# Three whole weight slots in a two-layer diffusion backbone: the low part overwrites the raw weights

## What is computed

```python
for i in range(2):
    m_l = silu(c) @ w_mod[i] + b_mod[i]            # shift, scale, gate, twice
    a_l = rmsnorm(x, norm_mix_g[i]) * (1 + sc1) + sh1
    # i == 0: z = a @ w_in -> q, k, v, g; chunked GLA both ways; o = rmsnorm(o) * silu(g); y = o @ w_out
    # i == 1: z = a @ w_in -> y, u; conv; r, i gates = sigmoid(u @ gate weights); linear scan; y = (h * gelu(y)) @ w_out
    x = x + g1 * y_l
    f_l = rmsnorm(x, norm_ffn_g[i]) * (1 + sc2) + sh2
    x = x + g2 * ((silu(f_l @ w1) * (f_l @ w3)) @ w2)
    # the context stream: the same in layer 0; in layer 1 it only feeds the scan
```

## Time and profile before

| | |
|---|---|
| median of three runs | 1799.82 us |
| the profiled execution | 1797.24 us |
| its span | 1795.3 us |
| PE busy | 1668.3 us (93%) |
| POOL busy | 603.3 us, of which 582.9 in `low` |
| ACT busy | 516.1 us, of which 192.4 in `high` |
| DVE busy | 609.2 us |
| granted PE clock, mean | 0.964 of full |
| DMA | 89 GB/s over the span |

### The profile page before, as it was taken

One profiled execution on the slowest core, in us unless ns is written; L12 is line 12 of the kernel. 1 busy time (PEld: TensorE's weight loads), 2 busy tenths in 40 slices (PEclk: granted clock), 3 DMA queues, 4 the chain that ended last, 5 costly groups with the idle time before them and its releaser, 6 DMA issues. The chain is left out here.

```text
span 1795.3 us, 22539 instructions
## 1 busy us (share of the span) xinstructions
PE 1668.3 (93%) x9980; PEld 1400.0 (78%) x9980; DVE 609.2 (34%) x700; ACT 516.1 (29%) x559; POOL 603.3 (34%) x434
## 2 busy tenths in 40 slices
PE   4799999998979999999999998899986799999997
PEld 2587888886868888888888887688865688888886
DVE  3733343434351121012110214758786412012122
ACT  3524141413132110111111113377772321122122
POOL 1221212212313233323322335244373355444453
PEclk9899999999989999999999999899997899999999
DMA  7242323223214332233322332022122132333322
GB/s 286 72 118 71 95 71 95 71 71 90 87 35 127 109 118 85 66 109 111 113 83 71 113 96 74 24 71 70 49 69 71 47 94 96 95 107 102 94 76 76
DMA packets 197492, 160.63 MB, mean 89 GB/s; under 512 B 7202, under 2 KB 193940, under 8 KB 197396
## 3 DMA queue, kind: packets, MB, share of 16 engines
q1 hardware_dynamic: 197396, 159.20, 28.7%
HBM read 157.08 MB, written 2.10 MB: 89 GB/s over the span
## 5 line engine op out<-in xcount | busy, mean ns | idle before, releaser
L490 POOL TENSOR_TENSOR w_lo<-raw,w_hi 128x512 fp32r<-128x512 f32 (+1 forms) x404 | 582.9, 1473 | 1165.1 <-ACT w_hi L918 1165.1
L534 PE MATMUL duo<-a_hi,w_hi 128*128 128x512 f32 (+1 forms) x1664 | 503.2, 363 | 52.9 <-DVE a_lo L1300 19.1
L540 PE MATMUL duo<-a_hi,w_lo 128*128 128x512 f32 (+1 forms) x1664 | 494.1, 357 | 0.0
L537 PE MATMUL duo<-a_lo,w_hi 128*128 128x512 f32 (+1 forms) x1664 | 493.0, 357 | 0.0
L534 PEld LDWEIGHTS duo<-a_hi,w_hi 128*128 128x128 f32 x1664 | 275.8, 192 | 116.4 <-issue 51.4
L918 ACT ACTIVATE w_hi<-raw 128x2048 fp32r<-128x2048 f32 (+1 forms) x101 | 192.4, 1905 | 590.4 <-PE duo L540 590.3
L537 PEld LDWEIGHTS duo<-a_lo,w_hi 128*128 128x128 f32 x1664 | 275.8, 192 | 47.7
L540 PEld LDWEIGHTS duo<-a_hi,w_lo 128*128 128x128 f32 x1664 | 274.4, 192 | 46.2
L1491 DVE TENSOR_TENSOR hid<-duo,gate 128x1024 f32<-128x1024 f32 (+1 forms) x33 | 33.5, 1043 | 540.3 <-PE duo L540 540.3
L534 PE MATMUL duo<-h_hi,w_hi 128*128 128x512 f32 (+1 forms) x528 | 160.8, 358 | 0.1
L540 PE MATMUL duo<-h_hi,w_lo 128*128 128x512 f32 (+1 forms) x528 | 158.8, 355 | 0.0
(11 more groups left out here) (211 smaller groups left out, 1502.5 us busy)
## 6 DMA issues: line engine op xcount, KB each, us to landing
raw<-in_ffn_w_dram SPq DMA_DIRECT2D x120, 512.0 KB, 4.9
mod_ring<-in_w_mod_dram SPq DMA_DIRECT2D x80, 512.0 KB, 5.2
raw<-in_gla_w_in_dram SPq DMA_DIRECT2D x24, 512.0 KB, 4.6
mod_first<-in_w_mod_dram SPq DMA_DIRECT2D x8, 1024.0 KB, 15.0
raw<-in_lru_w_in_dram SPq DMA_DIRECT2D x16, 512.0 KB, 4.2
raw<-in_ffn_w_dram SPq DMA_DIRECT2D x16, 384.0 KB, 3.8
raw<-in_gla_w_out_dram SPq DMA_DIRECT2D x8, 512.0 KB, 4.8
raw<-in_lru_w_out_dram SPq DMA_DIRECT2D x8, 512.0 KB, 4.5
```

The source lines that it names most:

```text
L490: pool.tensor_tensor(w_lo[b][:, k:k + 2, 0:cols], raw[b][:, k:k + 2, 0:cols], w_hi[b][:, k:k + 2, 0:cols].bitcast(F32), ALU.subtract).then ...
L534: pe.matmul(tile_out(ps, t, part, n), wh, act_hi[:, k, s:s + n], start=opens, stop=False, skip_group_check=True)
L537: pe.matmul(tile_out(ps, t, part, n), wh, act_lo[:, k, s:s + n], start=False, stop=False, skip_group_check=True)
L540: mm = pe.matmul(tile_out(ps, t, part, n), wl, act_hi[:, k, s:s + n], start=False, stop=last, skip_group_check=True)
```

## The change

Three slots instead of two. A slot is now a `raw` buffer, which the low part overwrites in place, and a `w_hi` buffer: 3 x 16 KB, the same 48 KB. `load` of chunk ch now waits until PE is done with chunk ch - 3. `high` waits for the load alone. The wait of `high` for `y_done` in an LRU block moves down to the GELU that reads the result. `low` handles a 768-row chunk in three instructions, not four, and rounding covers no more than the chunk has. The order of all the programs stays.

```diff
-        counts.append((counts[ch - 2] if ch >= 2 else 0) + (64 if name[0] == "lg" else 32))
+        counts.append((counts[ch - 3] if ch >= 3 else 0) + (64 if name[0] == "lg" else 32))
...
-        raw = [place(f"raw{b}", [P, 8, 256], F32, W_AT + 8 * KB * b) for b in range(2)]
-        w_hi = [place(f"w_hi{b}", [P, 8, 256], F32R, W_AT + 8 * KB * (2 + b)) for b in range(2)]
-        w_lo = [place(f"w_lo{b}", [P, 8, 256], F32R, W_AT + 8 * KB * (4 + b)) for b in range(2)]
+        raw = [place(f"raw{b}", [P, 8, 256], F32, W_AT + 8 * KB * b) for b in range(3)]
+        w_hi = [place(f"w_hi{b}", [P, 8, 256], F32R, W_AT + 8 * KB * (3 + b)) for b in range(3)]
+        w_lo = [place(f"w_lo{b}", [P, 8, 256], F32R, W_AT + 8 * KB * b) for b in range(3)]
...
+        HEIGHT = [6 if name[0] == "w2" and name[2] == 2 else 8 for name in CH]
+        LOWS = list(itertools.accumulate([0] + [h // 2 for h in HEIGHT]))
+        USERS = [("tlow" if name == "gate1" else name + (3,) if name[0] == "lg" else name) for name in CH]
...
-                if ch >= 2:
-                    sp.wait_ge(lo_ready, 4 * (ch - 1))
+                if ch >= 3:
+                    used = USERS[ch - 3]
+                    if used[0] == "ly" and used[1] < BLOCKS - 1:
+                        sp.wait_ge(y_done, used[1] + 1)
+                    else:
+                        wait_done(sp, used)
                 for dst, src in pieces:
-                    sp.dma_start(dst, src).then_inc(raw_loaded[ch % 2], 16)
+                    sp.dma_start(dst, src).then_inc(raw_loaded[ch % 3], 16)
...
-                for k in range(0, 8, 2):
+                for k in range(0, HEIGHT[ch], 2):
...
-            def high(name, q_before=None, cols=256, rows=8):
+            def high(name, cols=256):
...
                 act.wait_ge(raw_loaded[b], LOADED[ch])
-                if q_before is not None:
-                    wait_done(act, q_before)
-                act.activation(w_hi[b][:, 0:rows, 0:cols], raw[b][:, 0:rows, 0:cols], ACT.Copy).then_inc(hi_ready, 1)
+                act.activation(w_hi[b][:, 0:HEIGHT[ch], 0:cols], raw[b][:, 0:HEIGHT[ch], 0:cols], ACT.Copy).then_inc(hi_ready, 1)
...
                 if not last:
-                    act.wait_ge(y_done, n + 1)
                     high(("lg", n + 1))
                     round_u(n + 1)
...
                 act.wait_ge(scanned, n + 1)
+                act.wait_ge(y_done, n + 1)
                 for t, ps in enumerate((mod_psum, vec_psum)):
```

More of the change, by code:

```diff
@@ L1 @@
+import itertools
 from contextlib import ExitStack
@@ L267, in build @@
         vec_turned, vec_ready, cs_ready = sem("vec_turned"), sem("vec_ready"), sem("cs_ready")
-        raw_loaded = [sem(f"raw_loaded{b}") for b in range(2)]
+        raw_loaded = [sem(f"raw_loaded{b}") for b in range(3)]
         hi_ready, lo_ready = sem("hi_ready"), sem("lo_ready")
@@ L328, in load @@
                 ch = CH[name]
-                if ch >= 2:
-                    sp.wait_ge(lo_ready, 4 * (ch - 1))
+                if ch >= 3:
[4 more added lines that the diff above has]
+                        wait_done(sp, used)
                 for dst, src in pieces:
-                    sp.dma_start(dst, src).then_inc(raw_loaded[ch % 2], 16)
+                    sp.dma_start(dst, src).then_inc(raw_loaded[ch % 3], 16)
             def columns(name, w, col, rows=8):
-                r = raw[CH[name] % 2]
+                r = raw[CH[name] % 3]
                 v = w.rearrange("(k p) n -> p k n", p=P)
@@ L378, in qk_load @@
             def qk_load(h):
-                r = raw[CH[("qk", h)] % 2]
+                r = raw[CH[("qk", h)] % 3]
                 load(("qk", h), (r[:, :, 0:P], qk[:, :, 0, bass.ds(h * P, P)]),
@@ L435, in gate_columns @@
             def gate_columns(n):
-                r = raw[CH[("lg", n)] % 2]
+                r = raw[CH[("lg", n)] % 3]
                 load(("lg", n), *[(r[:, 4 * g + 2 * d:4 * g + 2 * d + 2], w[0, d, n].rearrange("(k p) j -> p k j", p=P))
@@ L486, in low @@
             def low(ch, cols=256):
-                b = ch % 2
+                b = ch % 3
                 pool.wait_ge(hi_ready, ch + 1)
-                for k in range(0, 8, 2):
+                for k in range(0, HEIGHT[ch], 2):
                     pool.tensor_tensor(w_lo[b][:, k:k + 2, 0:cols], raw[b][:, k:k + 2, 0:cols],
@@ L520, in chunk_wait @@
                 pe.wait_ge(hi_ready, CH[name] + 1)
-                pe.wait_ge(lo_ready, 4 * (CH[name] + 1))
+                pe.wait_ge(lo_ready, LOWS[CH[name] + 1])
             def tile_out(ps, t, part, n):
@@ L526, in tile_row @@
             def tile_row(chunk, name, parts, act_hi, act_lo, rows, k, t, k0=0, begin=None):
-                ps, hi, lo = duo(name), w_hi[CH[chunk] % 2], w_lo[CH[chunk] % 2]
+                ps, hi, lo = duo(name), w_hi[CH[chunk] % 3], w_lo[CH[chunk] % 3]
                 last = k == rows - 1
@@ L686, in v_matmuls @@
                 duo_wait(q)
-                hi, lo = w_hi[CH[q] % 2], w_lo[CH[q] % 2]
+                hi, lo = w_hi[CH[q] % 3], w_lo[CH[q] % 3]
                 for tau in range(TT):
@@ L847, in gate_tiles @@
                 chunk_wait(("lg", n))
-                hi, lo = w_hi[CH[("lg", n)] % 2], w_lo[CH[("lg", n)] % 2]
+                hi, lo = w_hi[CH[("lg", n)] % 3], w_lo[CH[("lg", n)] % 3]
                 for gi in range(4):
@@ L874, in y_tiles @@
                     pe.wait_ge(mod_ready, 12)
-                hi, lo = w_hi[CH[("ly", n)] % 2], w_lo[CH[("ly", n)] % 2]
+                hi, lo = w_hi[CH[("ly", n)] % 3], w_lo[CH[("ly", n)] % 3]
                 for t, ps in enumerate((mod_psum, vec_psum)):
@@ L984, in _ @@
                 square(n, n, TOK)
-            high("gate1", None, P)
+            high("gate1", P)
             prep(0, 0, BOTH)
@@ L995, in _ @@
             moved(act.activation(t_low[:, LAT:TOK], duo("tlow")[0:64, 2, 0:CTX], ACT.Copy), "tlow")
-            high(("v", 0), "tlow")
+            high(("v", 0))
             def o_scales(h):
@@ L1044, in _ @@
                     row_copy(s - 1, 1)
-                high(("g", h), ("qk", h))
+                high(("g", h))
                 act.preload_act_table_set("silu_and_others")
@@ L1049, in _ @@
                 moved(act.activation(v_tok[:].rearrange("p t n -> p (t n)"), flat(("v", h)), ACT.Copy), ("v", h))
-                high(("qk", h + 1) if h < HEADS - 1 else ("out", 0, 0), ("v", h))
+                high(("qk", h + 1) if h < HEADS - 1 else ("out", 0, 0))
                 wait_done(act, ("kt", h))
@@ L1055, in _ @@
                 act.preload_act_table_set("natural_log_exp_and_others")
-                high(("v", h + 1) if h < HEADS - 1 else ("out", 0, 1), ("g", h))
+                high(("v", h + 1) if h < HEADS - 1 else ("out", 0, 1))
             def split_out(layer, parts):
@@ L1077, in residual_loop @@
                     if ahead is not None:
-                        high(ahead, name)
+                        high(ahead)
                     if of == ("out", 0) and n == 3:
@@ L1096, in ffn @@
                         for name in (w1, w3):
-                            high({v: k for k, v in CH.items()}[CH[name] + 2], name)
+                            high({v: k for k, v in CH.items()}[CH[name] + 2])
                         if layer == 0:
@@ L1102, in ffn @@
                         for b in range(2):
-                            high(("w2", 1, part, 2 + b), ("w2", 1, part, b))
+                            high(("w2", 1, part, 2 + b))
                     else:
@@ L1160, in lru_block @@
                 sigmoids(n, 1)
-                high([("lu", 2), ("lu", 3), ("ly", 3), ("out", 1, 1)][n], ("lg", n, 3))
+                high([("lu", 2), ("lu", 3), ("ly", 3), ("out", 1, 1)][n])
                 steps.wait()
@@ L1189, in lru_block @@
                     block_input(("lu", n + 2))
-                    high(("ly", n + 1), ("lu", n + 2))
+                    high(("ly", n + 1))
                 else:
@@ L1194, in lru_block @@
                     moved(act.activation(last_y[:], part_psum(y, 0), ACT.Gelu_apprx_tanh), y)
-                    high(("out", 1, 0), y)
+                    high(("out", 1, 0))
             act.wait_ge(lruc_ready, 1)
             block_input(("lu", 0))
-            high(("lg", 0), ("lu", 0))
+            high(("lg", 0))
             round_u(0)
             block_input(("lu", 1))
-            high(("ly", 0), ("lu", 1))
+            high(("ly", 0))
             for n in range(BLOCKS):
```

## The result

The changed kernel takes 1838.05 us, the median of four runs (1830.89 to 1842.38), against 1801.73 us (1797.18 to 1805.04, four runs) for the kernel before. The ratio is 1.0199, with a 95% interval of 1.0156 to 1.0243: some 36 us slower, or 28 to 44 by the interval. The direction and the place of the loss are as forecast; the size is not, it lies above the range. The profiled execution is one of the longer ones of its four, 1840.85 us with a span of 1838.9, so between the two profiled executions there are 43.6 us to explain.

A forecast was written before the change was run, and what follows sets the result against it. PE, busy 93% of the span, was taken as the bound, so only its idle time counts. + 18.0 + 8.4 + 6.0 - 7.7 - 4.2 = + 20.5 on 1797.24 gave 1818 us, range 1803 to 1831.

The forecast's parts named there:

- SP's queue in the heads: In the heads, modulation pieces stand behind loads that now wait longer in SP's program; this and single layer 1 places matter.
- Pieces 4 and 5: Heads 0 to 2: stuck behind g_load, which waits for g(h); 6.0 us a head, 18.0 in all.
- pieces 2 and 3: Four heads: stuck behind the load that waits for v(h); 8.4 us in sum, between 0 and 10.4, no added clock loss.
- `out` 2: Layer 1: ACT rounds this chunk earlier, PE's 5.3 us wait goes, with 2.4 of clock; gain 7.7 us.
- the three ends: Ends of `out` 0, FFN 0 and `out` 1: POOL no longer runs beside DVE's sum of squares; gain 4.2 us.
- the four LRU waits: PE's other four chunk waits (2.45, 2.49, 2.50, 4.74 us) stay, since none of the orders on ACT and POOL changes.
- the bound on `out` 3: Layer 1: this chunk is late next, ready at 1384.1 against 1384.7 needed; a possible loss of 1 us.
- rounding really is free everywhere: Rival: all five chunk waits, 17.5 us, vanish with three clock dips, giving 1801, about no change; chance 0.10.
- the pieces are hidden: Rival: other PE work fills the gap ahead of the pieces, the heads cost nothing, giving 1785; chance 0.07.
- the clock behind pieces 4 and 5: Three heads: idle PE loses its granted clock, slowing the work behind; 2.0 us each, 6.0 in all, bounds 0 and 2.6.
- 8.9 us for the landing of four DMAs: In the heads, the second piece lands 8.9 us after the first of four DMA issues, read off the earlier trace.
- The rival "worse": Pieces 2 and 3 and the clock dips at upper bounds, gain only 5.3: + 40.5 us, 1838; chance 0.10.

The follow-up runs named there:

- e3: The changed kernel with g_load moved behind pieces 4 and 5 and v_load behind pieces 2 and 3 in SP's program: 1791.60 us, ratio 0.9946.
- e6: The kernel before, two slots, with two SP waits added in the heads: v_load(h + 1) waits for v(h), g_load(h + 1) for g(h): 1842.56 us.
- e9: The changed kernel with unneeded matmuls in heads 0 to 2, 46 ahead of piece 4 and 10 between pieces 4 and 5: 1822.10 us.
- e4: The changed kernel with 36 unneeded matmuls ahead of the slot of pieces 4 and 5 in heads 0 to 2: 1830.98 us.
- e8: The changed kernel with one of g_load's two DMAs ahead of pieces 4 and 5 and the other behind them: 1832.11 us.
- e5: e3 with the old wait of `high` put back, so rounding of chunk ch waits until PE is done with chunk ch - 2: 1800.76 us.

## Why the prediction was right in kind and wrong in size

The time was forecast at 1818 us within 1803 to 1831 and is 1838.05.

**Right: where the loss is.** "What matters is SP's queue in the heads" holds: in e3 the order alone takes away all but 6.3 of the 52.8 us that the heads had lost, and e6 makes the loss in the old kernel. Pieces 4 and 5 did wait in three heads, pieces 2 and 3 in four, pieces 0 and 1 nowhere. The idle time at pieces 4 and 5 is 18.5, close to the forecast's 18.0 a little by luck: the second pieces landed up to 1.4 us later after the first issue than forecast, and the slowed matmuls of the first piece covered part of that. The slots as wholes, which is what the forecast had priced at 18.0, cost 22.0.

**Right: the gains.** `out` 2 gave 8.1 for 7.7, the three ends 4.3 for 4.2, the four LRU waits stayed, `y_done` and the in-place subtraction cost nothing that can be seen, both FFNs stayed covered, and the bound on `out` 3 did not bite. The rival "rounding really is free everywhere" falls by the 12.2 us that stayed, "the pieces are hidden" by the 41.8. For the ends the Trainium skill, "SBUF — State Buffer" ("Who interferes with whom"), says that the two engines block each other fully. The prediction made up to about 8 us of it; with this case's 1.46 us a POOL instruction it is 2 x 1.46 x 3 = 8.8. That is an upper bound, so the measured 4.3 does not speak against the rule. It agrees with the row's 0.70 us an addition.

**Wrong: the clock behind pieces 4 and 5, 2.0 us each.** This is the step "What runs behind it is small work, so I take 2.0 each ... and bounds of 0 and 2.6". It is 4.6, 4.7 and 5.0 behind the slots, and some 1.1 more in each slot, where 32 matmuls that took 1.08 us now take 1.08 for each 16. I sized it from the earlier trace rows, where PE regained its full clock 5.2 us after it resumed, and took that duration for a property of a dip. In these heads the low clock lasted over 11 us after PE resumed, so the gate product and the one with `att` ran slow from end to end. The price of a dip was how much work ran under it, and I had the durations of that work in hand: 2.85 + 2.86 us, which at half the clock cost 2.6 and 1.9 more. The upper bound was the worse error, since it was taken from the one place whose work behind is different. e9 shows the term by itself: with the clock kept up, 14.3 us of slower work are gone, not 6.

**Wrong: pieces 2 and 3, 8.4 us and "I take nothing more" for the clock.** They cost 16.5. Piece 3 was forecast at 123.2 in head 0 and was used at 125.77: 1.5 is the shift from the start, which is no part of this term, 1.0 the landing (next point). The landing adds 1.0, 1.1, 2.3 and 0.9 in the four heads, and the dip that was there got deeper: PEclk is 0.50 from 124 to 129 us where it had been 0.81 from 120 to 129. In all there are 12.7 us of added idle time and 3.8 of slower work.

**Wrong: 8.9 us for the landing of four DMAs.** It is 9.9, in both rows shown above, and in the seven slots in order 9.9, 9.9, 10.0, 10.3, 11.2, 9.2 and 9.8. The 8.9 came from the earlier trace rows, where the issues followed one another just as closely, so the row was apt and still 1 us short; over seven slots that makes 8.0 us. The Trainium skill's figures, "DMA: Bandwidth & Descriptors" ("Where 436 GB/s comes from", "Latency and other measured facts"), had given 7.9, an estimate; the trace lies further from it than from the row, and by it the forecast would have been worse still.

**The rival "worse", at 1838,** names the measured time, but not by its terms: it had 10.4 + 9.6 at pieces 2 and 3 where 16.5 was measured, 18 at pieces 4 and 5 for 22.0, 7.8 of clock for 14.3, and a gain of 5.3 for 12.4. Most of its errors cancel. It was the case in which everything stood at its bound, and I gave it 0.10 and ended the range below it; three terms of the same sign, all leaning on the same two rows, go wrong together and should have been held inside the range.

## What to carry to other kernels

When a wait is lengthened at an engine that issues DMAs, list what stands behind it in that engine's program and price each by "released, plus all transfers ahead of it, minus needed". If an urgent transfer stands there, put it first: here that turned 2% slower into 0.5% faster, and the hoisted rounding made 1% of it. Where a gap on PE brings the clock down, as those of 4.7 to 6.4 us ahead of pieces 4 and 5 did here, price it as its idle time plus the work behind it at half the clock, taking that work from the timeline of the same place.

## What the runs showed of the chip that I had not expected

- The granted clock stays low for different times: full again 5.2 us after PE resumed in the earlier trace rows, over 11 us at 163.05 in head 0, with PE busy nearly throughout in both. Why the second is longer isn't settled. The length of the wait alone does not decide it: after 4.73 us of it in head 2 (PE resumed at 366.56) the clock is 0.50 until 379, by the window below, while after 6.51 us at `out` 0 of layer 1 (PE resumed at 1419.72) its mean from 1424 to 1426 is 0.97 again. What differs in these traces is the work that PE resumed with, the modulation, gate and `att` products in the one and products of 128x512 in the other; no run changes that alone. e4 and e9 show that the low clock goes when the wait is filled, and that 36 fillers before the first piece were too few in heads 0 and 2 and enough in head 1.

```profile
366.00:379.00 13.00, 11.60 (x50) 7.04 (x51) 0.00 (x0) 2.00 (x4) 3.03 (x3) 0.50 0.39 108
```

- Four DMAs of 512 KB in a row, after a quiet queue: the last is used 9.2 to 11.2 us after the first issue (seven places); three: 7.3 to 8.0 (three places in e8).
- POOL's subtraction got faster by the moment at which it runs, not by working in place. Its instructions of 128x512 took 579.1 us before and 519.9 after, at 1478 and 1360 ns each (392 of them after, 400 before); in e5, in place too but at the old moment, they take 1482. That it meets DVE less is likely, and was not tested by itself.

```profile
L498 POOL TENSOR_TENSOR w_lo<-raw,w_hi 128x512 fp32r<-128x512 f32 x392 | 519.9, 1360 | 1223.1 <-ACT w_hi L924 1223.1
```

```profile
L499 POOL TENSOR_TENSOR w_lo<-raw,w_hi 128x512 fp32r<-128x512 f32 x392 | 569.1, 1482 | 1141.8 <-ACT w_hi L931 1141.8
```
